# The opening of a two-block network kernel: two of eight modulation slabs applied by TensorE, and squares, bias rows and constants in another order

## The reference

```
cs = silu(c)                                   # c: 1 x 1024
mod = cs @ mod_w[0] + mod_b[0]                 # 1024 x 6144
sh_m, sc_m = mod[:, :1024], mod[:, 1024:2048]
h = rmsnorm(x, norm_mix[0]) * (1 + sc_m) + sh_m
u = h @ lru_w_in                               # 1024 x 2560, then conv, gates, scan, ...
```

## Time and profile before

| | us |
|---|---|
| median of three timed runs (1728.89 to 1734.77) | 1733.55 |
| profiled execution | 1728.39 |
| its span, first to last instruction | 1726.7 |
| TensorE busy | 1678.9 (97%) |
| VectorE busy | 1277.1 (74%) |
| ScalarE busy | 901.1 (52%) |
| mean granted clock of TensorE, as a share | 0.995 |

### The profile page before, as it was taken

One profiled execution on the slowest core, in us unless ns is written; L12 is line 12 of the kernel. 1 busy time (PEld: TensorE's weight loads), 2 busy tenths in 40 slices (PEclk: granted clock), 3 DMA queues, 4 the chain that ended last, 5 costly groups with the idle time before them and its releaser, 6 DMA issues.

```text
span 1726.7 us, 27296 instructions
## 1 busy us (share of the span) xinstructions
PE 1678.9 (97%) x10474; PEld 1497.9 (87%) x10474; DVE 1277.1 (74%) x1573; ACT 901.1 (52%) x1240; POOL 110.5 (6%) x161
## 2 busy tenths in 40 slices
PE   6999999999999999999999999999999999999997
PEld 4987999999899998888898888888888899788887
DVE  7999788868765449777775877687777775777676
ACT  4567433457543445434578534466434468644445
POOL 3110211100200000000012000000000003000000
PEclk9999999999999999999999999999999999999999
DMA  9994799948554544554441455544454452355542
GB/s 380 333 335 162 285 369 363 375 167 306 177 205 179 194 176 153 195 197 177 174 162 69 173 207 182 194 163 179 175 205 180 173 181 74 135 209 181 194 170 86
DMA packets 61920, 353.73 MB, mean 205 GB/s; under 512 B 6522, under 2 KB 9738, under 8 KB 27792
## 3 DMA queue, kind: packets, MB, share of 16 engines
q1 hardware_dynamic: 40064, 281.24, 44.5%
q0 software_dynamic: 18384, 66.66, 10.5%
q10 hardware_dynamic: 3392, 4.72, 0.9%
HBM read 349.45 MB, written 3.15 MB: 204 GB/s over the span
## 4 chain that ended last, share of the span: by engine, by line
PE 83%; DVE 10%; issue 2%; ACT 2%; DMA 1%; POOL 1%; DVEq 0%; ACTq 0%; POOLq 0%
PE banks L537 18%; PE banks L506 16%; PE banks L508 15%; PE banks L507 15%; PE banks L538 9%; DVE w_lo L1618 3%; PE banks L551 2%; PE banks L553 2%; PE banks L552 2%; PE banks L711 1%; DVE shared L1640 1%; PE banks L644 1%; DVE work L2019 1%; DMA work<-in_mods 1%; POOL work L493 1%
## 5 line engine op out<-in xcount | busy, mean ns | idle before, releaser
L537 PE MATMUL banks<-a_both,w_hi 128*128 128x512 f32 x1408 | 500.9, 400 | 2.5 <-DVE a_both L1691 2.2
L1901 DVE TENSOR_TENSOR w_lo<-raw,w_hi 128x2048 fp32r<-128x2048 f32 x144 | 329.8, 2290 | 178.4 <-ACT w_hi L1207 178.3
L538 PE MATMUL banks<-a_both,w_lo 128*128 128x256 f32 x1408 | 396.2, 281 | 0.0
L506 PE MATMUL banks<-a_both,w_hi 128*128 128x256 f32 x1240 | 354.9, 286 | 7.8 <-DVE a_both L1778 2.7
L1207 ACT CAST w_hi<-raw 128x2048 fp32r<-128x2048 f32 x144 | 274.2, 1906 | 161.9 <-PE banks L508 127.6
L508 PE MATMUL banks<-a_both,w_lo 128*128 128x256 f32 x1240 | 352.5, 284 | 0.0
L507 PE MATMUL banks<-a_both,w_hi 128*128 128x256 f32 x1240 | 352.5, 284 | 0.0
L537 PEld LDWEIGHTS banks<-a_both,w_hi 128*128 128x128 f32 x1408 | 265.6, 189 | 68.7 <-issue 4.0
L1618 DVE TENSOR_TENSOR w_lo<-raw,w_hi 128x2048 fp32r<-128x2048 f32 x122 | 278.6, 2290 | 62.7 <-ACT w_hi L1066 62.5
L538 PEld LDWEIGHTS banks<-a_both,w_lo 128*128 128x128 f32 x1408 | 267.5, 190 | 1.3
L1066 ACT CAST w_hi<-raw 128x2048 fp32r<-128x2048 f32 x121 | 229.7, 1909 | 39.9 <-PE banks L508 25.9
(11 more groups left out here) (265 smaller groups left out, 2137.7 us busy)
## 6 DMA issues: line engine op xcount, KB each, us to landing
raw<-in_stream SPq DMA_DIRECT2D x266, 1024.0 KB, 4.8
shared<-in_mods POOLq DMA_DIRECT2D x104, 512.0 KB, 6.6
grow<-in_rows POOLq DMA_DIRECT2D x12, 512.0 KB, 3.9
work<-in_mods POOLq DMA_DIRECT2D x8, 512.0 KB, 9.9
bias_rows<-work ACTq DMA_DIRECT2D x1, 2048.0 KB, 22.4
x<-in_x_t SPq DMA_DIRECT2D x1, 1024.0 KB, 6.0
x<-in_x_d ACTq DMA_DIRECT2D x1, 1024.0 KB, 6.4
work<-bias_rows ACTq DMA_DIRECT2D x1, 1024.0 KB, 15.5
```

Source lines behind the costliest of these rows:

```text
L506: pe.matmul(out, w_h, v_h, start=start, stop=False, skip_group_check=True)
L537: pe.matmul(out[:, :], w_h, a_both[:, c].rearrange("p k s -> p (k s)"), start=(c == 0), stop=False, skip_group_check=True)
L538: mm = pe.matmul(out[:, 0:S], w_l, a_hi[:, c, :], start=False, stop=(c == CH - 1), skip_group_check=True)
L1901: dve.tensor_tensor(w_lo[:, slot, :], raw[:, slot, :], w_hi[:, slot, :].bitcast(F32), ALU.subtract).then_inc(lo_ready, 1)
```

## The change

- The first modulation group has 6 slabs (12 halves) on VectorE. Slabs 6 and 7 (`DIRECT`) are loaded whole into a part of `work` that the bias rows use later (`mix_slots`), on GpSimd's queue behind halves 1 and 5. TensorE multiplies them by `cs[:, k]` directly, 16 products with one column each, into bank 7, and the column products are added to that, now with one column of ones each.
- On TensorE the order is: norm sums, direct products, bias rows, column products, 5 products that keep it busy, the stream.
- On ScalarE the root stands before the bias copies, and the cast of slab 2 behind the normed chunks.
- On VectorE the constants stand behind the split of slab 2; slabs 0 and 1 are both split ahead of the columns and the gain.
- SyncE issues slabs 0, 1 and 2 after 3, 5 and 11 modulation steps. The loads of the next group wait until the first group is finished.

```diff
@@ sync
-            sp.wait_ge(mod_step, 9)
             for s in range(RING):
+                sp.wait_ge(mod_step, (3, 5, 11)[s])
                 sp.dma_start(raw[:, s, :], stream[s]).then_inc(landed[s], 16)
@@ gpsimd
             for u in range(2 * MOD_RING):
                 pool.dma_start(mod_slots[u], mod_half(u)).then_inc(mod_landed[u], 16)
+                if u in (1, 5):
+                    i = u // 4
+                    pool.dma_start(mix_slots[i], mods[len(MOD_ORDER) // 2 + i]).then_inc(mix_landed[i], 16)
...
-                pool.wait_ge(mod_step, u - 2 * MOD_RING + 1)
+                pool.wait_ge(mod_step, u - 2 * MOD_RING + 1 if u < 3 * MOD_RING else max(u - MOD_RING + 1, 3 * MOD_RING))
@@ tensor
             pe.wait_ge(const_ready, 1)
+            norm_stat(N_MIX0)
+
+            pe.wait_ge(cs_ready, 1)
+            for i, k in enumerate(DIRECT):
+                pe.wait_ge(mix_landed[i], 16)
+                for m in range(16):
+                    pe.matmul(bank[7][:, 32 * m:32 * m + 1], mix_slots[i][:, m * P:(m + 1) * P], cs[:, k:k + 1],
+                                   start=(i == 0 and m == 0), stop=False, skip_group_check=True)
+
             pe.wait_ge(rbb_ready, 2)
...
-            norm_stat(N_MIX0)
 
             pe.wait_ge(row_ev, HEADS)
-            pe.wait_ge(mod_step, 14)
-            keep_warm(8)
-            mod_reduce(G_MIX0, 7)
-
-
-            need_slab(B_WIN)
-            keep_warm(9)
+            pe.wait_ge(mod_step, MOD_LAST[G_MIX0, 1])
+            for m in range(16):
+                mm = pe.matmul(bank[7][:, 32 * m:32 * m + 1], mod_sums(G_MIX0)[:, m * P:(m + 1) * P], ones[:, 0:1],
+                               start=False, stop=True, skip_group_check=True)
+            mm.then_inc(mod_cols, 1)
+
+            keep_warm(5)
@@ scalar
             squares(N_MIX0, lambda c: x_in[:, c, :], lambda c: None)
+            rsqrt(N_MIX0, D)
             for h in range(HEADS):
                 act.wait_ge(row_mm, h + 1)
                 act.copy(bias_rows[:, h, :], bank[h % 2][:, :]).then_inc(row_ev, 1)
-            rsqrt(N_MIX0, D)
+            split_to(2)
+            normed_hi(A_MIX0, a_out, lambda c: modcol(G_MIX0, c))
             split_to(RING)
-            normed_hi(A_MIX0, a_out, lambda c: modcol(G_MIX0, c))
@@ vector
+            dve.wait_ge(cs_ready, 1)
+            for kc in range(8 - len(DIRECT)):
+                mod(G_MIX0, kc)
+            root(N_MIX0, D)
+            split_to(2)
+            mod_columns(G_MIX0, 7)
+            scale_of(0, G_MIX0, CH, COL_AT["norm_mix"])
+            dve.wait_ge(scale_ready, 1)
+            normed(A_MIX0, N_MIX0, x_src, lambda c: scale1[:, c:c + 1], a_h, a_l, lambda c: modcol(G_MIX0, c))
+            split_to(RING)
             dve.wait_ge(lam_act, 2)
...
@@ order of the slabs
+DIRECT = (6, 7)
+MOD_ORDER = (both(*((g, k) for g in (G_MIX0, G_A0) for k in range(8) if g != G_MIX0 or k not in DIRECT)) + [(G_B0, k, h) for h in range(2) for k in range(8)]
```

More of the change, by code:

```diff
@@ L326, in mod_slot @@
             n = MOD_RING
-            return (u % (2 * n), u // (2 * n) + 1) if u < 4 * n else (u % n, u // n - 1)
+            return (u % (2 * n), u // (2 * n) + 1) if u < 3 * n else (u % n, u // n)
         def mod_sums(g):
             return {G_A1: mod_third, G_MIX1: mod_fourth}[g] if g in (G_A1, G_MIX1) else mod_acc[:, g % 2, :]
+        mix_landed = [sem(f"direct_mod_landed{i}") for i in range(len(DIRECT))]
+        mix_slots = [area(6144, 2048), area(8192, 2048)]
         scale_ready = sem("scale_ready")
@@ L461, in _ @@
                 nc.gpsimd.memset(mod_sums(g), 0.0).then_inc(acc_zero, 1)
-            mod_loads(MOD_LAST[G_B0, 1], 16 * G_B1 + MOD_RING)
+            mod_loads(MOD_LAST[G_B0, 1], MOD_LAST[G_A1, 1] + MOD_RING)
             row_load(U_MOBA)
-            mod_loads(16 * G_B1 + MOD_RING, 16 * MOD_GROUPS)
+            mod_loads(MOD_LAST[G_A1, 1] + MOD_RING, len(MOD_ORDER))
             row_load(U_FFN1)
@@ L1997, in _ @@
             assert lam_n[0] == LAM_STEPS
[L1998 to L2008, removed]
             mod_half(4)
@@ L2198, in _ @@
             mod(G_B1, 7)
-            assert steps[0] == 16 * MOD_GROUPS
+            assert steps[0] == len(MOD_ORDER)
             split_to(B_FFN1 + 1)
@@ L2469 @@
 IN_LOOP = (G_KV, G_MIX1, G_A1)
-MOD_ORDER = (both(*((g, k) for g in (G_MIX0, G_A0) for k in range(8))) + [(G_B0, k, h) for h in range(2) for k in range(8)]
+DIRECT = (6, 7)
+MOD_ORDER = (both(*((g, k) for g in (G_MIX0, G_A0) for k in range(8) if g != G_MIX0 or k not in DIRECT)) + [(G_B0, k, h) for h in range(2) for k in range(8)]
              + both(*((g, k) for k in range(8) for g in IN_LOOP)) + both(*((G_B1, k) for k in range(8))))
@@ L2560, in mod_slabs @@
         yield np.concatenate([groups[g][P * k:P * (k + 1), MOD_HALF * h:MOD_HALF * (h + 1)] for g, k, h in MOD_ORDER[u:u + 2]], axis=1)
+    for k in DIRECT:
+        yield groups[G_MIX0][P * k:P * (k + 1)]
 def columns(a):
```

## The result

The changed kernel takes 1741.8 us (median of 5 runs, 1739.86 to 1745.19); the kernel before, beside it on the same chip, 1729.83 (5 runs, 1728.89 to 1734.77). The ratio is 1.0065, 95% interval 1.0049 to 1.0080: slower by 8.5 to 13.8 us, under 1% but clear of the spread. Forecast: slower, 1743 (1734 to 1749). The profiled execution has a span of 1738.2 us, 11.5 above that of before.

What follows compares the result with a forecast made beforehand. The opening, up to the first stream product, was taken to bound the gain or loss. Bias rows delayed behind direct slab 1 (+10.0 us) and work moved behind normalizing (+2.1) gave 12.1 us: 1743 us, range 1734 to 1749.

Steps and rivals of the forecast that it cites:

- What bounds: Opening: modulation halves' landings, VectorE's fixed work behind the last, and TensorE's and ScalarE's prior work set the stream's start.
- Rival C: After the opening: TensorE's later waits take the loss back, no more than 2 us; no chance of its own given.
- Bytes: Modulation loads: same bytes, direct slab 1 landing at 22.5; last multiply-add ending at 34.5, +1.2 us if it decides.
- Sixteen direct products: TensorE behind direct slab 1: 16 one-column products take 5.9 us at the slow pace (3.5 to 7.0), ending at 28.4.
- Bias rows: TensorE behind the direct products: bias rows at the slow level, 14.6 us with their copies, ending at 43.0.
- Rival A: Bias stage at full clock, copies ending at 33.8: loss 3.1 us, 1734, not slower; chance 0.13.
- Casts and splits: ScalarE and VectorE behind the copies: cast to 44.9, splits to 47.1 and 49.3; normalizing at 49.7, +10.0 us.
- Column products: TensorE behind the bias copies: 5.9 us, ending at 48.9, hidden behind VectorE's splits.
- Moved behind the normalizing: Slab 2's cast and VectorE's lambda steps before the first convolution: 1.5 + 3.5 - 2.9 = +2.1 us.
- Warm-up: Five instead of 17 products keeping TensorE busy before the stream: 0, bounds -1.7 and +1.7 us.
- Base: Starting time: 1740.5 from the profiled 1728.39, 1745.7 from the timed median 1733.55; the middle, 1743, was taken.
- The sum: Whole loss: 10.0 us at normalizing plus 2.1 us behind it, 12.1 us.

Runs made afterwards that it cites:

- all-halves-first run: The changed kernel with all three first stream slabs issued after nine modulation steps, as before: 1741.65 us, ratio 1.0057 to the kernel before.
- 128-row runs: The changed kernel with bias operands zero-filled from 33 to 128 rows: 1736.05 us; with warm-up products between the direct slabs too, 1732.43 us (one run).
- constants-in-front run: The changed kernel with VectorE's constants ahead of its first multiply-add and slab 2's cast ahead of the normed pieces: 1739.6 us, ratio 1.0046.
- one-column look at the kernel before: The kernel before with one column in its column products: 1731.87 us, ratio 1.0004.

## Why the prediction was right

- *What bounds.* That the first stream product sets the end, and the loss passes through undiminished: right in the main, 13.34 us at the first convolution, 11.5 at the end of the profile and 12.0 in the medians; the difference goes with the falls of the level told above, not with waits that took it back. Rival C did not happen.
- *Bytes.* Direct slab 1 landed at 21.96 (22.5 predicted). The last multiply-add ended at 34.6 (34.5) and did not decide, as the all-halves-first run shows.
- *Sixteen direct products.* The term mis-sized: 5.9 us predicted from the ratio of two load durations, 6.99 measured, the upper bound (7.0). The pace of a load doubles, 0.218 us against 0.113 (6.99 and 3.63 us over 32). The Trainium skill (TensorE: Matmul & The Clock Gate, section LDWEIGHTS) gives a load by its columns alone, 128 / 1.2 = 107 ns. The first direct slab (0.113) comes near that, the second (0.218) does not; by the page's figure, as an estimate, the bias rows would have started 3.6 us earlier.
- *Bias rows.* Low level, 14.02 us, last copy ending at 43.55 (43.0): right. Rival A fell. The ground given, that 33-row products do not raise the level, is what the 128-row runs isolate. The Trainium skill (TensorE: Matmul & The Clock Gate, section on why this matters for your kernels) says that keeping TensorE continuously busy brings the full clock. The trace agrees for the 128-row bias products (at 1.00 from 32.4 on), and disagrees for the 33-row ones (0.50 over 14 us without a gap) and for one-column products (1.00 to 0.50 at 33.2 without a gap).
- *Casts and splits.* First split 45.45 (44.9), both done at 49.9 (49.3), VectorE's wait 9.56 us (some 9): right. *Column products.* "Hide behind that": wrong by 0.68 us. With the doubled pace they took 6.99 instead of 5.9 and ended at 50.6, behind the splits. Normalizing +11.35 instead of +10.0: 0.5 from the later end of the copies (the slab 0.5 early, its products 1.1 long), 0.7 from the column products, 0.1 in small pieces.
- *Moved behind the normalizing.* 13.34 - 11.35 = 2.0 us (2.1): right, and the constants-in-front run took 2.2 off.
- *Warm-up.* Priced at 0. The stream began inside the low stretch, which ended 1.1 us after its first product, where before it ran low for 3.3 us. By an estimate, half of the difference, 1.1 us, is gained, in the bounds; VectorE was late anyway, so it did not show.
- *Base.* The middle of the two bases, 1731.0, is what all 94 runs of before have as their median; a base from either number alone would have been 2.6 off. The sum, 12.1, is 1.2 low at the first convolution (13.34) and 0.1 from the medians' difference (12.0). That it fits the end so well is luck in part: two terms were too small, and the falls of the level further on gave about as much back in the profile.

## What to carry to other kernels

Work that another engine's queue stands behind (here eight copies ahead of the casts) is expensive to move behind a transfer, however small it looks: what it costs is the landing plus its own time less the slack of that queue. A product's time in an opening depends on the clock level, and the level depends on the form of the products that run, so read at both levels the pace of each form that you move. Put independent work of an engine in front of the result that it would wait for, and see that nothing else then holds the next engine: the split moved into the wait for the column products was part of the only version that beat the kernel before, and a warm-up that was too long hid its effect at the first product.

## What the runs showed of the hardware

- Products over 33 rows (33x512), 14 us without a gap, leave the granted clock at 0.50; the same over 128 rows, zeros in 95, had it at 1.00 from 32.4 on, having started at 28.08 at 0.50.
- The granted clock fell from 1.00 to 0.50 in a gapless run of one-column products (at 33.2, begun at 28.34), and in one of 32-column products (at 33.9, begun at 28.62).
- A bare weight load with a narrow product goes every 0.113 us at 2.4 GHz and every 0.218 us at 1.2 GHz.
- Later in the kernel the level falls for about 3.4 us at places where TensorE has short waits, in some executions and not in others: in before at 1189.1, after waits of 1.91 and 0.77 us, and in the kernel after not at the same place, with the same two waits. So two single profiles differ by some us for no reason of the kernels'.
- The opening differs by execution too. The one-column look at the kernel before had its last half landed 1.3 us later than in the profile of before and its column products at the low level, and its first convolution at 58.73 instead of 55.45; its span was 1730.7 us against 1726.7, and the timed runs showed no difference.
